# Inverting triangular matrices in 32x32 tiles, and loading most modulation weights under the first RWKV head loop

## What is computed

```python
def modulation(cond, w_mod, b_mod):             # one w_mod of 1024 x 6144 for each layer
    m = jax.nn.silu(cond) @ w_mod + b_mod
    return jnp.split(m[..., None, :], N_MOD, axis=-1)
# every layer: x <- LN(alpha*x + gate*sublayer(x*(1+scale)+shift)), twice (mixer, MLP)

# DeltaNet, for each chunk of 64 tokens; the RWKV scan has the same inverse inside
tmat = lax.linalg.triangular_solve(eye + low, jnp.broadcast_to(eye, low.shape),
                                   left_side=True, lower=True)
```

## Time and profile before

| | before |
|---|---|
| median of 3 runs (range) | 6480.66 us (6477.11 to 6486.7) |
| the profiled execution's own time | 6486.38 us |
| its span, first to last instruction | 6484.6 us |
| mean granted TensorE clock | 0.901 of 2.4 GHz |
| busy: PE, PEld, DVE, ACT, POOL | 84%, 76%, 39%, 29%, 9% |

### The profile page before, as it was taken

The page is one execution under the profiler, slowest core; times in us unless marked ns, Lnnn a source line. Parts: engine busy times, 40 slices in busy tenths (PEclk is TensorE's granted clock), DMA queues, the critical chain, the costliest instruction groups (busy, mean ns, idle before and its releaser), DMA issues. The chain is left out here.

```text
span 6484.6 us, 149579 instructions
## 1 busy us (share of the span) xinstructions
PE 5473.3 (84%) x66220; PEld 4914.0 (76%) x66220; DVE 2521.4 (39%) x4363; ACT 1883.0 (29%) x3891; POOL 614.3 (9%) x1064
## 2 busy tenths in 40 slices
PE   6678999969996578699986788779968899995998
PEld 2377888859995356599885677679948688885998
DVE  0232555434333422343422454343453345543333
ACT  1022334332222222322222333232222243333222
POOL 0002223200000000000000322100000223220000
PEclk7787999989997678899998798889989899997999
DMA  9521000012212100122132211112202100001221
GB/s 407 251 104 42 21 24 22 9 47 88 74 45 80 37 21 11 61 77 77 39 123 63 57 42 36 63 52 78 71 32 99 40 14 23 24 9 64 78 74 53
DMA packets 105672, 426.36 MB, mean 66 GB/s; under 512 B 19208, under 2 KB 34824, under 8 KB 74568
## 3 DMA queue, kind: packets, MB, share of 16 engines
q1 hardware_dynamic: 91920, 388.70, 17.2%
q10 hardware_dynamic: 13248, 30.15, 1.2%
HBM read 369.81 MB, written 49.26 MB: 65 GB/s over the span
## 5 line engine op out<-in xcount | busy, mean ns | idle before, releaser
L356 PE MATMUL bank<-src_hi,ring_hi 128*128 128x320 f32 x4032 | 934.9, 314 | 334.9 <-DVE ring_lo L348 334.9
L356 PEld LDWEIGHTS bank<-src_hi,ring_hi 128*128 128x128 f32 x4032 | 686.4, 191 | 338.4 <-issue 338.2
L356 PE MATMUL bank<-src_lo,ring_hi 128*128 128x320 f32 x4032 | 931.2, 313 | 0.0
L356 PE MATMUL bank<-src_hi,ring_lo 128*128 128x320 f32 x4032 | 929.9, 312 | 0.0
L356 PEld LDWEIGHTS bank<-src_lo,ring_hi 128*128 128x128 f32 x4032 | 686.3, 191 | 0.0
L356 PEld LDWEIGHTS bank<-src_hi,ring_lo 128*128 128x128 f32 x4032 | 685.1, 191 | 0.0
L348 DVE TENSOR_TENSOR ring_lo<-ring,ring_hi 128x2048 fp32r<-128x2048 f32 x190 | 435.0, 2289 | 512.1 <-ACT ring_hi L344 511.3
L562 ACT ACTIVATE stage<-bank 128x320 f32<-128x320 f32 x512 | 196.1, 435 | 1398.9 <-PE bank L356 1398.9
L356 PE MATMUL bank<-hidden_hi,ring_hi 128*128 128x320 f32 x2048 | 466.7, 309 | 0.0
L356 PE MATMUL bank<-hidden_lo,ring_hi 128*128 128x320 f32 x2048 | 466.7, 309 | 0.0
L356 PE MATMUL bank<-hidden_hi,ring_lo 128*128 128x320 f32 x2048 | 466.7, 309 | 0.0
(11 more groups left out here) (348 smaller groups left out, 8851.7 us busy)
## 6 DMA issues: line engine op xcount, KB each, us to landing
ring<-w_mlp SPq DMA_DIRECT2D x128, 1024.0 KB, 4.8
mod_ring<-w_mod SPq DMA_DIRECT2D x48, 2048.0 KB, 11.9
ring<-rw_wrkv SPq DMA_DIRECT2D x24, 1024.0 KB, 4.9
ring<-dn_win SPq DMA_DIRECT2D x16, 1024.0 KB, 5.2
rkv<-stage ACTq DMA_DIRECT2D x48, 320.0 KB, 2.2
r_k<-rkv SPq DMA_DIRECT2D x32, 320.0 KB, 3.6
src<-mixed SPq DMA_DIRECT2D x32, 320.0 KB, 8.1
dn_proj<-stage ACTq DMA_DIRECT2D x32, 320.0 KB, 2.2
```

What stands on the lines that cost most here:

```text
L356: last = self.nc.tensor.matmul(acc[h][:, 0:HALF], wt[:, n % 2, k, m * P:(m + 1) * P], x[:, k, h * HALF:(h + 1) * HALF], start=first and q ...
```

## The change

It does two things:

- `NS` is 256, so a slab is 1 MB and there are 96. `modulation` does the first 8 (`MOD_FIRST`, the scale and shift that layer 0 needs at once). The other 88 are passed to the head loop of layer 0: twelve levels of each pair (`Q_MOD`, every even q) multiply one slab, two (`Q_COLS`, q = 11 and 23) turn six slabs' rows into columns. There are two slab buffers instead of one.
- The matrices are inverted in four 32x32 diagonal tiles of the array (`quads`) where there were two of 64x64 (`rows`). A product of levels 0 to 3 is sixteen matmuls of 32x32x32 where it was eight of 64x64x64. The last level joins two 32-blocks: eight matmuls for y, eight copies and eight products for the lower block of the transpose; the upper block is copied by ACT with a mask (`TB_EVEN`) one level earlier. `first_inverse` makes X and its transpose by PE, 32 matmuls, straight from `lt`; POOL's product for the transpose is gone, and DVE masks both (`near`) where ACT copied one.

```diff
-NS = 512
+NS = 256
 MOD_STEPS = 6 * D // NS
 MOD_BLOCKS = NS // P
 MOD_RING = 3
-MOD_FIRST = DEPTH * MOD_STEPS
+MOD_FIRST = 2 * D // NS
...
-Q_MOD, Q_COLS, MOD_GROUP = (1, 4, 7, 12, 15, 18), (9, 21), 3
+Q_MOD, Q_COLS, MOD_GROUP = tuple(range(0, 24, 2)), (11, 23), 6
...
+                def load_mods(c, first, last):
+                    for n in range(c * len(Q_MOD) + first, min(c * len(Q_MOD) + last, MODS)):
+                        if n >= 2:
+                            sp.wait_ge(s["m_ps"], mod_turn[(n - 2) // len(Q_MOD), Q_MOD[(n - 2) % len(Q_MOD)]] + 1)
+                        sp.dma_start(mod_slab[:, n % 2, :, :].rearrange("p k n -> p (k n)"),
+                                     g.d["w_mod"][first_slab + n]).then_inc(s["mod_loaded"][n % 2], 16)
...
-                        pool.wait_ge(s["lt_ready"], n + 1)
-                        l0 = table[:, TB_L0I:TB_L0I + C].unsqueeze(1).to_broadcast([P, 4, C])
-                        nc.gpsimd.tensor_tensor(x0[:, 1, :, :], lt[:, n % 2, :, :], l0, ALU.mult).then_inc(s["x0t_ready"], 1)
...
-                    if level == LEVELS - 1 and prepares(t):
-                        act.wait_ge(s["x0_ps"], t + 2)
-                        nc.scalar.copy(flat(x0[:, 0, :, :]), four(x_bank)).then_inc(s["x0_copied"], 1)
...
+                            last = nc.scalar.copy(flat(xx[:, level % 2, 1, :, :]), four(xt_bank))
+                            if level == LEVELS - 2:
+                                last = nc.scalar.activation(tt[:, t % 2, :, 0:Q], four(xt_bank).rearrange("p (u c) -> p u c", u=4),
+                                                            ACT.Identity, scale=table[:, TB_EVEN:TB_EVEN + 1])
...
                 def first_inverse(n):
-                    pe.wait_ge(s["x0t_ready"], n + 1)
+                    pe.wait_ge(s["lt_ready"], n + 1)
                     for u in range(4):
-                        for hr in rows:
-                            last = nc.tensor.matmul(x_bank[hr, u * C:(u + 1) * C], x0[hr, 1, u, :], i64[hr, :], start=True, stop=True)
+                        for f, o in zip(quads, own):
+                            nc.tensor.matmul(x_bank[f, u * Q:(u + 1) * Q], lt[f, n % 2, u, o], i64[f, o], start=True, stop=True)
+                    for u in range(4):
+                        for f, o in zip(quads, own):
+                            last = nc.tensor.matmul(x_bank[f, (4 + u) * Q:(5 + u) * Q], i64[f, o], lt[f, n % 2, u, o],
+                                                    start=True, stop=True)
...
                     for u in range(4):
-                        for hr in rows:
-                            last = nc.tensor.matmul(y_bank[hr, u * C:(u + 1) * C], lt[hr, t % 2, u, :], x[hr, 0, u, :],
-                                                    start=True, stop=True)
+                        if level < LEVELS - 1:
+                            for f, o in zip(quads, own):
+                                last = nc.tensor.matmul(y_bank[f, u * Q:(u + 1) * Q], lt[f, t % 2, u, o], x[f, 0, u, :],
+                                                        start=True, stop=True)
+                        else:
+                            for f, f_low in (quads[0:2], quads[2:4]):
+                                last = nc.tensor.matmul(y_bank[f_low, u * Q:(u + 1) * Q], lt[f, t % 2, u, Q:C], x[f, 0, u, :],
+                                                        start=True, stop=True)
...
+                    for u in range(4):
+                        for f in quads:
+                            last = nc.tensor.matmul(xt_bank[f, u * Q:(u + 1) * Q], y[f, u, :], x[f, 1, u, :], start=True, stop=True)
                     last.then_inc(s["xt_ps"], 1)
...
+                        near = table[:, TB_L0I:TB_L0I + C].rearrange("p (w c) -> p w c", w=2).unsqueeze(2).to_broadcast([P, 2, 4, Q])
+                        nc.vector.tensor_tensor(x0[:, :, :, :], x_bank[:, 0:8 * Q].rearrange("p (w u c) -> p w u c", w=2, u=4), near,
+                                                ALU.mult).then_inc(s["x0_copied"], 1)
```

More of the change, by code:

```diff
@@ L264, in _ @@
                         kr = slice(32 * (k % 4), 32 * (k % 4) + 32)
-                        last = nc.tensor.matmul(bank[n % 2][kr, :], silu32[:, k, :], ring[:, n % MOD_RING, k, :], start=(k < 4),
+                        last = nc.tensor.matmul(bank[n % 2][kr, 0:NS], silu32[:, k, :], ring[:, n % MOD_RING, k, :], start=(k < 4),
                                                 stop=(k >= 4))
@@ L277, in _ @@
                         act.wait_ge(s["cols_ready"], n - 1)
-                    nc.scalar.copy(rows[:, n % 2, :], bank[n % 2][:, :]).then_inc(s["rows_ready"], 1)
+                    nc.scalar.copy(rows[:, n % 2, :], bank[n % 2][:, 0:NS]).then_inc(s["rows_ready"], 1)
             @block.vector
@@ L292, in _ @@
                 dve.wait_ge(s["cols_added"], len(slabs))
-                scales_plus_one(nc, g, [(layer, piece) for layer in range(DEPTH) for piece in (1, 4)])
+                scales_plus_one(nc, g, [(0, 1)])
 def modulate_blocks(dve, nc, g, ready, scale, shift, done=None):
@@ L992, in rwkv_heads @@
         col = lambda i, n: hcols[:, i, n:n + 1]
-        four = lambda bank: bank[:, 0:4 * C]
+        four = lambda bank: bank[:, 0:4 * Q]
+        quads = [slice(n * Q, (n + 1) * Q) for n in range(4)]
+        own = [slice(n % 2 * Q, (n % 2 + 1) * Q) for n in range(4)]
         flat = lambda ap: ap.rearrange("p u c -> p (u c)")
@@ L1315, in next_inverse @@
                         pe.wait_ge(s["xt_copied"], LEVELS * t + level)
[L1316 to L1322, removed]
-                    for u in range(4):
-                        for hr in rows:
-                            last = nc.tensor.matmul(xt_bank[hr, u * C:(u + 1) * C], y[hr, u, :], x[hr, 1, u, :],
-                                                    start=True, stop=True)
+                    for u in range(4):
+                        for f in quads:
+                            last = nc.tensor.matmul(x_bank[f, u * Q:(u + 1) * Q], x[f, 1, u, :], y[f, u, :], start=True, stop=True)
+                    last.then_inc(s["x_ps"], 1)
+                    for u in range(4):
+                        for f in quads:
+                            last = nc.tensor.matmul(xt_bank[f, u * Q:(u + 1) * Q], y[f, u, :], x[f, 1, u, :], start=True, stop=True)
                     last.then_inc(s["xt_ps"], 1)
@@ L1465, in modulation_piece @@
                         pe.wait_ge(s["m_free"], mod_turn[c, q])
[L1466 removed]
+                        pe.wait_ge(s["mod_loaded"][slab_at(c, q, MODS) % 2], 16 * (slab_at(c, q, MODS) // 2 + 1))
                         for k in range(NB):
                             kr = slice(32 * (k % 4), 32 * (k % 4) + 32)
[L1469 removed]
+                            last = nc.tensor.matmul(m_bank[kr, 0:NS], silu32[:, k, :], mod_slab[:, slab_at(c, q, MODS) % 2, k, :], start=(k < 4), stop=(k >= 4))
                         last.then_inc(s["m_ps"], 1)
```

162 lines of the change are left out of this document (98 added, 64 removed).

## The result

| | before | after |
|---|---|---|
| median of 4 runs (range) | 6478.89 us (6473.72 to 6486.7) | 6817.93 us (6788.02 to 6832.13) |
| ratio, 95% interval | | 1.0516 [1.0478, 1.0555] |
| the profiled execution | 6486.38 us | 6788.02 us |

What follows compares the result with a forecast made beforehand. DMAs loading weights were taken to bound modulation, PE's own order the RWKV head loops, PE's work and waits DeltaNet. Terms -218 + 86 + 41 + 56 - 84 - 25 + 25 = -119 us gave about 6365 us median, range 6235 to 6520.

Steps and rivals of the forecast that it cites:

- modulation removed: Modulation stage up front: only 8 slabs of 1 MB stay, some 28 us of 246; -218 us.
- slab matmuls: First head loop: 88 slabs on PE's path at 0.98 us each, +86 us.
- column matmuls: First head loop: 176 blocks x 2 x 0.111 us and 16 changes of size, hidden under DMAs before; +41 us.
- waits for the bank: First head loop: PE's pieces wait until ACT has read the slab's sums, 8.3 us a pair; +56 us.
- inversion, both head loops: Smaller tiles -2.7, size changes +1.8, waits -0.2: net -1.1 us a slot, 40 slots twice; -84 us.
- DeltaNet: DeltaNet head stage: up to 2.7 us x 20 could come from smaller tiles; half taken, -25 us.
- clock: Head loops: PE's waits and drains lower its clock, 2% of 1300 us; +25 us.
- I take 16, as the modulation stage shows four tiles of 32 columns side by side: Inversion: a 32x32 program matmul takes 16 ns with four tiles in turn; upper bound 29 ns.
- if the second loop is not shorter: Sign of being wrong: the second head loop, without slabs, was to be some 40 us shorter.
- the tiles don't pack, or instructions don't arrive fast enough: Rival, inversion: a program matmul stays at 29 ns, +290 us, 6655; past 7200 at 58 ns; chance 0.13.
- More waits than summed: Rival: bank steps cost 0.5 us more each, or clock 0.9 in both loops; +100 to +130 us; chance 0.17.
- Changes of size free: Rival: changes between 64x64 and 32x32 cost nothing instead of 0.12 us each; 6220 us; chance 0.1.

Runs made afterwards that it cites:

- experiment 1: Changed kernel with all modulation up front again (48 slabs of 2 MB), 32x32 inversion kept: 6818.06 us, ratio 1.0512.
- experiment 3: As experiment 1, but at levels 0 to 3 each weight load takes two units' columns, half the matmuls omitted, inverse not computed: 6403.26 us, ratio 0.9884.
- experiment 4: Kernel before with 1024 matmuls of 32x32, then 512 of 64x64, without waits, put ahead of the first slab's matmuls: 6566.98 us, one run.

## Why the prediction was wrong, point by point

| term | forecast, us | measured, us |
|---|---|---|
| modulation removed | -218 | -220 |
| slab matmuls | +86 | +97 |
| column matmuls | +41 | +43 |
| waits for the bank | +56 | +42 |
| these three and the rest of the first loop | +183 | +197 |
| inversion, both head loops | -84 | +306 (experiment 1) |
| DeltaNet | -25 | +17 (+26 in experiment 1) |
| clock | +25 | contained in the two above; granted 0.86 and 0.88 in the loops, 0.76 in DeltaNet |

- **The failed step** is "I take 16, as the modulation stage shows four tiles of 32 columns side by side". As the speed of a run it held: 0.28 us for 16 matmuls of the program. As a rate for a stage it did not: the arrival of instructions stands in the sum at nothing. 64 of them at 16 ns use up a packet in 1.0 us, and packets come 3.6 us apart. The 7 ns starts that it rested on are four of 16 in a slab, and a slab with its column matmuls was 24 matmuls and 24 loads in 5.1 us (246 / 48), a fifth of a packet: a stage that asks for few instructions can't show how fast they come.
- The forecast was 390 us off in the head loops (306 + 84), 4.9 us a slot, where 512 more instructions at 14.1 ns are 7.2 us. Part of the arrival stayed hidden, since 910 instructions left room (12.8 us of a slot's 19.4); on the other side the clock fell. In the second loop idle time rose by 98 us (47 to 145) and busy time by 60 (731 to 791), with 229 us at 1.2 GHz instead of 51. How much each would cost without the other was not tried. The prediction had "if the second loop is not shorter" among its signs of being wrong; it is 159 us longer.
- DeltaNet is a small part of it, and less clear. Its "issue" waits are 15 us, of 17 lost, where it had none; it also has 296 us at 1.2 GHz instead of 176. In experiment 3 the stage took 571 us, 32 less than before.
- The rival *the tiles don't pack, or instructions don't arrive fast enough* (0.13) held the cause in its second half. Its evidence, twice the inversion's instructions and 413 packets, was on the table, but it was priced by what two tiles can do (29 ns, 6655) and not by packets. The kernel before gave a hint: in its second head loop 144 packets cover 778 us, 5.4 us each, and no two start less than 3.42 us apart. For 1422 instructions, 5.6 packets a slot, those 3.42 alone are 19.0 us, above the 18.3 that a slot was to take (778 / 40 less 1.1). It was no more than a hint: packets of the changed kernel start as little as 3.25 us apart, which would give 18.1. What was missing is a trace in which PE has nothing else to wait for, and experiment 4 made one.
- The Trainium skill's rule (TensorE: Matmul & The Clock Gate, "Wait — 56ns, not 53.3ns?"), that starts are never closer than about 25 ns, is not borne out across four tiles: L1342's 32 matmul instructions start 9 ns apart. A sum by it would have come nearer the result, for a reason that is not at work.
- *More waits than summed* (0.17): the steps of the bank cost less, not more. Its other branch, a clock of 0.9 in both loops, did come, with 0.86 and 0.88, but with the stops of PE and not with waits for the bank: experiment 1 has 0.88 without a slab. *Changes of size free* (0.1): no run tested the 0.12 us alone. With nearly all of the arrival out of the way (experiment 3) the loop was 26 us shorter, where half of 84, 42, was forecast. That kernel runs other matmuls in the inversion, so it says only that the changes were probably not underpriced by much.
- The slab move's own sum, -35 us, came out at -13 in the median and -20 in its stages (-217 and +197): the two kinds of matmuls cost 12 more and the rest of the loop 15 (the loop has 98 us at 1.2 GHz instead of 68), the waits 14 less.
- Range: 6235 to 6520 cut off the packing rival, with its 0.13. The time is 300 us above the range.

## What to carry to other kernels

Before splitting matmuls into smaller tiles, count instructions, not columns: a 32-bit matmul is four here, 256 instructions make a packet, and a stream without waits got one packet in 3.6 us. If a stage's instructions times 14 ns come near its time (20.1 us of 19.4 here), tiles that raise the count lose, whatever each could do, and one load of weights for more columns gains. When moved work costs more than its matmuls, read the order of the engine that frees its bank and of the queue that issues its loads: moving a copy took 47 us off the stage here, moving an issue 73.

## What the runs showed of the hardware

- PE's instructions came in packets of 256. When PE had nothing else to wait for (experiment 4), its runs started 3.46 to 4.01 us apart, 3.62 in the mean: 2.3 to 3.0 us from a packet's start to PE's run, 1.0 to 1.5 from there to the next packet's start. 442 instructions ran before the first stop.
- Where PE stopped for instructions, 108 us in all in 131 waits, its granted clock was 0.88 in the loop that had 0.97 before; it was 0.95 where the stops were down to 16 us and the tile changes stayed.
- A stream of 64x64 matmuls on 64 columns, 63 ns each, ran without a stop: it used 256 instructions in 4.0 us, little more than the 3.62 of a packet.
